# The order of scores and values on TensorE in three attentions: two key tiles at a time in place of one

## The reference, cut to what matters

```python
# first block, layers 0 and 1: 8 query heads, 2 key heads, 1024 own keys + 256 context keys
def dense_attn(q, k, v):
    s = jnp.einsum("bqkgd,bskd->bkgqs", q, k).astype(jnp.float32)
    p = jax.nn.softmax(s, axis=-1).astype(v.dtype)
    o = jnp.einsum("bkgqs,bskd->bqkgd", p, v)
...
# (layer 0 also sends the 256 context queries through dense_attn, against the context keys alone)

# second block: 8 heads of 64, causal, with a bias from the summed forget gates
def fox_attention(q, k, v, log_f):
    ...
        sc = jnp.einsum('bqhd,bkhd->bhqk', qb, kb).astype(jnp.float32) * scale
        bias = c[:, :, start:end, None] - c[:, :, None, :end]
        sc = jnp.where(mask, sc + bias, NEG_BIG)
        pr = jax.nn.softmax(sc, axis=-1).astype(v.dtype)
        outs.append(jnp.einsum('bhqk,bkhd->bqhd', pr, vb))
```

## Time and profile before

| | |
|---|---|
| median of 3 runs | 4016.35 us (4014.44 to 4030.46) |
| the profiled execution | 4012.03 us |
| its span, first to last instruction | 4010.2 us |
| TensorE busy | 3736.2 us, 93% of the span |
| VectorE, ScalarE, GpSimd busy | 1935.0, 1099.3, 1642.2 us (48%, 27%, 41%) |
| mean granted TensorE clock | 0.968 of full |

### The profile page before, as it was taken

One profiled execution on the slowest core, in us unless ns is written; L12 is line 12 of the kernel. 1 busy time (PEld: TensorE's weight loads), 2 busy tenths in 40 slices (PEclk: granted clock), 3 DMA queues, 4 the chain that ended last, 5 costly groups with the idle time before them and its releaser, 6 DMA issues. The chain is left out here.

```text
span 4010.2 us, 61305 instructions
## 1 busy us (share of the span) xinstructions
PE 3736.2 (93%) x26398; PEld 2848.3 (71%) x26398; DVE 1935.0 (48%) x2162; ACT 1099.3 (27%) x1544; POOL 1642.2 (41%) x897
## 2 busy tenths in 40 slices
PE   6999999889999899998999997888989999999998
PEld 5888544678778543777776776775577788888877
DVE  4442576552543565633559204435642662635542
ACT  3123344330223344411245212224500210101120
POOL 1332266543333366443347434502532344434433
PEclk9999799999999999999999999988999999999999
DMA  4011200034112100042211210020032111111111
GB/s 181 32 43 64 62 1 1 15 130 181 60 36 70 31 1 1 15 152 65 90 56 46 97 67 4 4 95 1 1 120 89 48 46 50 48 49 52 48 48 68
DMA packets 93747, 227.02 MB, mean 57 GB/s; under 512 B 28320, under 2 KB 37536, under 8 KB 92592
## 3 DMA queue, kind: packets, MB, share of 16 engines
q1 hardware_dynamic: 76096, 188.75, 13.7%
q10 hardware_dynamic: 17392, 34.48, 2.6%
HBM read 184.36 MB, written 38.83 MB: 56 GB/s over the span
## 5 line engine op out<-in xcount | busy, mean ns | idle before, releaser
L1760 PE MATMUL acc<-h_hi,weights_hi 128*128 128x512 f32 (+1 forms) x928 | 365.0, 393 | 8.5 <-DVE h_lo L1921 6.1
L1762 PE MATMUL acc<-h_hi,weights_lo 128*128 128x512 f32 (+1 forms) x928 | 339.7, 366 | 0.0
L1015 DVE TENSOR_REDUCE part_max<-aux 128x1 f32<-128x428 f32 (+5 forms) x468 | 252.8, 581 | 179.9 <-PE aux L856 130.2
L1761 PE MATMUL acc<-h_lo,weights_hi 128*128 128x512 f32 (+1 forms) x928 | 339.6, 366 | 0.0
L2441 PE MATMUL acc<-h_hi,weights_hi 128*128 128x512 f32 x672 | 274.3, 408 | 12.4 <-POOL weights_lo L2498 6.8
L3399 POOL TENSOR_TENSOR weights_hi<-weights,ones 128x1024 fp32r<-128x1024 f32 (+1 forms) x66 | 122.6, 1857 | 389.7 <-PE acc L3349 389.7
L3347 PE MATMUL acc<-h_hi,weights_hi 128*128 128x512 f32 x704 | 274.9, 390 | 6.5 <-DVE h_lo L555 4.8
L3349 PE MATMUL acc<-h_hi,weights_lo 128*128 128x512 f32 x704 | 274.6, 390 | 0.0
L3348 PE MATMUL acc<-h_lo,weights_hi 128*128 128x512 f32 x704 | 274.6, 390 | 0.0
L1935 DVE RECIPROCAL arena<-arena 128x512 f32<-128x512 f32 (+1 forms) x48 | 141.7, 2953 | 261.4 <-ACT arena L1898 261.4
L2443 PE MATMUL acc<-h_hi,weights_lo 128*128 128x512 f32 x672 | 263.8, 393 | 0.0
(11 more groups left out here) (464 smaller groups left out, 8635.5 us busy)
## 6 DMA issues: line engine op xcount, KB each, us to landing
weights<-in_w_in SPq DMA_DIRECT2D x44, 512.0 KB, 3.4
weights<-in_w_up SPq DMA_DIRECT2D x43, 512.0 KB, 3.5
arena<-in_w_mod SPq DMA_DIRECT2D x6, 2048.0 KB, 8.7
weights<-in_w_out SPq DMA_DIRECT2D x21, 512.0 KB, 5.2
weights<-in_w_mod SPq DMA_DIRECT2D x4, 2048.0 KB, 26.5
mixer_gates<-arena SPq DMA_DIRECT2D x32, 256.0 KB, 2.0
x_between<-arena ACTq DMA_DIRECT2D x16, 512.0 KB, 3.5
weights<-in_w_gates SPq DMA_DIRECT2D x16, 512.0 KB, 3.5
```

What stands on the lines that cost most here:

```text
L1015: nc.vector.tensor_reduce(part_max[:, b % 2, j, hh, i:i + 1], max_tile(m)[:, hh, 0:cw], AX_X, ALU.max, negate=True).then_inc(max_done, 1)
L1760: nc.tensor.matmul(out, w_hi[:, b, k, :], hi[:, k, cols], start=(k == 0), stop=False)
L1761: nc.tensor.matmul(out, w_hi[:, b, k, :], lo[:, k, cols], start=False, stop=False)
L1762: return nc.tensor.matmul(out, w_lo[:, b, k, :], hi[:, k, cols], start=False, stop=(k == KD - 1))
```

## The change

Only the layout of the list changes. The loop takes entries two by two: first the scores of both, then, for each of the two, the tasks of its slots and the values, as before.

```diff
-    for e in range(len(exps) + lag + 6):
-        if e < len(exps):
-            order.append(("scores", e))
-        order += tasks.get(2 * e, [])
-        if 0 <= e - lag < len(exps):
-            order.append(("values", e - lag))
-        ending = [b for b in range(len(blocks)) if 0 <= e - lag - blocks[b][1] <= 1]
-        order += [("out", b) for b in ending if blocks[b][1] + lag == e]
-        order += [("sums", b) for b in ending if blocks[b][1] + lag + 1 == e]
-        order += tasks.get(2 * e + 1, [])
+    for e0 in range(0, len(exps) + lag + 6, 2):
+        two = (e0, e0 + 1)
+        order += [("scores", e) for e in two if e < len(exps)]
+        for e in two:
+            order += tasks.get(2 * e, [])
+            if 0 <= e - lag < len(exps):
+                order.append(("values", e - lag))
+            ending = [b for b in range(len(blocks)) if 0 <= e - lag - blocks[b][1] <= 1]
+            order += [("out", b) for b in ending if blocks[b][1] + lag == e]
+            order += [("sums", b) for b in ending if blocks[b][1] + lag + 1 == e]
+            order += tasks.get(2 * e + 1, [])
```

## The result

The changed kernel takes 4046.06 us (median of 6 runs, 4030.21 to 4061.21) against 4016.55 us before (6 runs, 4014.04 to 4031.51): a ratio of 1.0075, 95% interval 1.0058 to 1.0092, so 0.75% slower. The forecast was 4042 us.

The account below looks back on a forecast made before the run. TensorE's issue order was taken to set the time. 36.4 us lost less 22.1 gained made 14 slower, plus 12 for the clock: 26 on 4012.03, 4038, and 4.3 for the median, so 4042; 8-in-10 range 4006 to 4066.

Parts of the forecast that it names:

- The signs named beforehand: Changed kernel's trace: mean clock in three windows about 0.93, TensorE's waits for VectorE up some 10 us or more.
- The joined scores: Attentions on TensorE: 107 more adjoining scores visits save 0.19 us each in switching, 20.3 us gained.
- the places: Attentions: 36 new spots where one maximum task follows another on TensorE and needs `aux` back from VectorE.
- The plain place: Order `SSMVMMVM`, 30 of 36 new places: third maximum task hands over at 3.45 us; 0.75 each, 22.5 lost.
- layer 1's places: Layer 1: 9 plain at 0.75 us each; 6 behind a block's last inversion at 0.15, 0.9 in all.
- The rows: Block starts: first scores 0.3 us late at 22 blocks, 6.6; 0.4 more behind a cast at 9, 3.6.
- The clock: New places: one in four followed by a 3.4 us stretch at half clock, 9 x 1.3 = 12 us lost.
- What was costed at nothing: Attentions: waits for exponentials, the buffer ring and GpSimd's additions, taken as covered; if GpSimd's failed, about 1 us per block end.
- the ring of three: Three probability buffers: exponential of e+1 must wait for values e-2, but 2 us of other work covers it; no cost.
- That the clock holds: Rival 1, whole kernel: no added clock falls, only the 14 us loss remains, 4030 us; chance 0.27.
- That the switches decide: Rival 2: joined scores and values gain 22.1 us and adjoining maxima cost little, 3994 to 4000 us; chance 0.12.
- A collapse beyond 4061: Rival 3: clock falls at two of three places, longer than one stretch, 4061 to 4093 us; chance 0.12.

Follow-up runs that it names:

- Spread: The changed kernel, with maximum tasks kept out of slots 4k+2 and sharing slots with inversions; 3994.30 us against 4013.94 before, ratio 0.9950.
- the last experiment: The changed kernel with the two layers' ring of probability buffers cut from 4 to 3; 4046.21 us against 4019.24 before the change, ratio 1.0077.
- adjoining alone: The old alternating order, with only the tasks of slot 2e+2 moved up behind those of 2e+1; 4057.59 us against 4019.24 before, ratio 1.0112.

## Why the prediction was right, and where it was not

**Direction, size, mechanism: right; the nearness of the sum is partly luck.** 4042 forecast, 4046 measured. The windows' 33.5 us split into 21 or 22 for the clock (56 to 58 us at half clock x 0.38) and 12 for the rest; the forecast had 12 and 14. The clock was taken 10 us too low. The 12 and 14 look alike only because errors offset: beside the clock the forecast's terms make some +6, +5 and +3 us for layer 0, layer 1 and the forgetting attention (with 8, 7 and 7 of its 22 rows), and the windows give 0, +3 and +10.

**The signs named beforehand.** The mean clock in the three windows is 0.94, where about 0.93 was named. TensorE's waits for VectorE's reductions rose by 8.0 us (4.4 to 7.9, 4.1 to 7.0, 2.3 to 3.9), a little under the 10 or more. Layer 0 did not get longer at all: the 255.00 us of the earlier trace rows are a shorter cut of the 258.86 shown above, and against those it took 258.69.

**The joined scores** (0.19 us each): right where it can be read, 2.06 us for both against a forecast of 2.07. The sum of 20.3 is not isolated by any run. Spread keeps them and loses the places, but its 20 us over all are 12 in the windows beside the clock. There values at the start of layer 0's blocks wait 7.0 us for inversions, 2.2 before, where the tasks now share slots with the inversions, and the rows cost something too, so 12 speaks neither for nor against 20.3.

**The plain place** (0.75 us): right to a hundredth at the place shown, with the third task at 3.45. Isolated in the old order the 34 places cost 19 us together, where the prices make 21.0 + 0.9: somewhat less, with layer 1's places the cheapest, at 0.4 each.

**The rows** (0.3, and 0.4 more behind a cast): about right for one, wrong in number. A plain one and one with the casts, in layer 1:

```profile
1412.79 0.64 PE L872 MATMUL aux<-ident_rounded,neg_max 128*1 128x128 f32 x8
...
1414.56 0.47 PE L891 MATMUL acc<-q_both_parts,k_twice 128*128 128x512 f32 x1
```

```profile
1376.77 0.64 PE L872 MATMUL aux<-ident_rounded,neg_max 128*1 128x128 f32 x8
...
1378.90 0.50 PE L891 MATMUL acc<-q_both_parts,k_twice 128*128 128x512 f32 x1 [0.48 <-ACT q_and_shift L950]
```

1.77 and 2.13 us from row to scores, where 1.82 and some 2.2 stood; a row and the values behind it take 1.58 when nothing is waited for, so 0.2 and 0.55 are lost. But the forecast counts 22 blocks. Written out, only 13 have nothing but one values between their row and their first scores: 7 in layer 1, 4 in the forgetting attention and 2 in layer 0. The other rows, most of layer 0's and three of the forgetting attention's, are issued well ahead of their block, and the scores that follow them belong to an earlier block and do not wait for them. One in layer 0:

```profile
539.51 0.64 PE L872 MATMUL aux<-ident_rounded,neg_max 128*1 128x128 f32 x8
539.98 0.45 PE L891 MATMUL acc<-q_both_parts,k_twice 128*128 128x512 f32 x1
```

With these prices the rows cost about 4 us in all, where 6.6 + 3.6 = 10.2 stood.

**The clock** ("one place in four, 9 x 1.3 = 12 us"): the mis-sized term. It measured 21 or 22 us, and 45 to 48 of the 56 to 58 us more at half clock lie in the forgetting attention, of which the prediction showed no row. I had priced its 7 places as the layers'. There three stretches of 10 us follow adjoining tasks, and three more of 7 to 10 us follow the gap for the next pair's casts. In the layers 29 places brought only one new fall, of 10 us, and 4 us of time. So the stretches were longer than the 3.4 us that I had priced, and fewer in the layers than the one place in six. Why the forgetting attention's places are so often followed by a fall is not shown: the values around them have fewer columns, its tasks have bias matmuls, and no run varies one of these alone.

**What was costed at nothing**: the ring of three in the layers costs 5 us in layer 0 and perhaps 3 in layer 1, as the last experiment shows, so the cover that the forecast trusted is not whole. What the forecast had no term for in the forgetting attention is the wait for the casts of the next pair. TensorE's waits there, after:

```profile
PE aux L857 <- issue: 7.1, 3, 2.9
PE acc L912 <- POOL total L1087: 4.9, 1, 4.9
```

Before they were 3.9 and 4.0 us: TensorE waits 3.2 us more for the casts over three pairs, and 0.9 us more for GpSimd's additions at the end. With adjoining alone the first is 5.4, so about half of the rise comes without two scores in a row. That the ring of three holds the casts back by way of the exponentials is my reading, not shown. These 4 us and the places' own 5 do not make up the 10 us beside the clock, less so with some 5 gained by joined scores; the rest is open.

**Layer 0** came out even (-0.2 us, with as much half clock). By the forecast's terms it should have lost 6. Some 3.5 of these are the rows that do not wait. For the other 2 or 3 us I have no run.

**Rivals.** That the clock holds is refuted by 0.85. That the switches decide is refuted for this order, by the full price of a place. With the places gone they may well decide: spread ran at 3994.30, though the 3994 to 4000 of that rival were given for another kernel. A collapse beyond 4061 did not come; one of the six runs took 4061.21.

## What to carry to other kernels

When an order is changed to join equal work, write out what else becomes neighbours: here 107 joined scores were worth an estimated 20 us, and 36 neighbouring users of one PSUM buffer, each up to 0.75 us and cheap to see beforehand, lost as much, and half-clock time on top. Fix the neighbours, not the idea: with the side tasks spread the same joining was 0.5% faster than before. Count each term in the written order, stage by stage: a row task that stands far ahead costs nothing, and a total can come out right by two stages that are wrong in opposite ways. And read rows from every stage that changes. The stage without one held most of the loss.

## What the runs showed of the hardware

In the forgetting attention TensorE at full clock waited 0.16 and 0.37 us within 2 us, and the granted clock then fell to 0.50 for 10 us; it did so at two of three places with the same waits, so the waits alone do not decide it. Filling these waits with matmuls of no use, 853 instead of 798 in the window, made that window 8.7 us shorter. The same fill made the two layers together 3.1 us longer, where little half clock was there to be won. Here useless work in a wait paid only where it gave full clock back.
